# A two-block network on one core: weights' rests before operands' rests in the first ff product, shorter norms, and products of ones in the waits of two norms

## The reference, cut to what matters

```python
def rmsnorm(x, g):
    y = xf * lax.rsqrt(jnp.mean(xf * xf, axis=-1, keepdims=True) + EPS)
    return y * g
# first block
h = rmsnorm(x, norm_mix_g)                 # "n1"
...                                        # seven projections, gating, convolution
x = x + einsum(m, w_out)
hf = rmsnorm(x, norm_ff_g)                 # "n2"
z = relu(einsum(hf, w_ff1))                # 1024 -> 4096
x = x + einsum(z * z, w_ff2)               # 4096 -> 1024
x = rmsnorm(x, norm_final_g)               # "between"
# second block
mod = silu(c) @ w_ada + b_ada              # six vectors of 1024
h = rms_norm(x, g_norm1) * (1 + scale1) + shift1      # "n3"
...                                        # attention, gated linear attention, out projection
h2 = rms_norm(x, g_norm2) * (1 + scale2) + shift2     # "n4"
...                                        # gated mlp with a convolution
return rms_norm(x, g_final)                # "final"
```

## Time and profile before

| | |
|---|---|
| median of three runs | 1570.07 us (1569.48 to 1571.84) |
| the profiled execution | 1571.68 us, of which the span is 1569.9 us |
| busy, share of the span | PE 96%, weight loads 76%, DVE 51%, ACT 36%, POOL 2% |
| mean granted clock of PE | 0.973 of full |
| the chain that ended last | PE 89%, DVE 4%, ACT 3%, issue 2%, DMA 1% |

### The profile page before, as it was taken

How to read it: one execution, slowest core, us unless ns; L and a number is a source line. 1 busy time by engine, 2 the same in 40 slices (tenths; PEclk the granted TensorE clock), 3 DMA queues, 4 the chain that set the end, 5 groups by cost and what they waited for, 6 DMA issues and landing times.

```text
span 1569.9 us, 18627 instructions
## 1 busy us (share of the span) xinstructions
PE 1510.3 (96%) x6586; PEld 1198.4 (76%) x6586; DVE 804.0 (51%) x1108; ACT 562.6 (36%) x759; POOL 28.6 (2%) x68
## 2 busy tenths in 40 slices
PE   6999999999999999999997998999898999999997
PEld 5887888888887788888886764555686888888885
DVE  7344221652455656656677535445357552663564
ACT  4343222323233313232244333433435541551342
POOL 1000000000000000000000000000000000000000
PEclk7999999999999999999998999999898999999998
DMA  5333323233222553545344120110022233323221
GB/s 169 106 101 101 105 82 107 81 107 105 82 85 78 186 186 121 187 160 187 120 162 146 54 81 27 38 43 28 27 82 79 91 103 101 100 87 107 80 81 53
DMA packets 135788, 158.15 MB, mean 101 GB/s; under 512 B 2513, under 2 KB 129071, under 8 KB 135743
## 3 DMA queue, kind: packets, MB, share of 16 engines
q1 hardware_dynamic: 129024, 131.08, 25.9%
q0 software_dynamic: 6240, 26.30, 5.0%
q10 hardware_dynamic: 479, 0.17, 0.0%
HBM read 155.44 MB, written 2.10 MB: 100 GB/s over the span
## 4 chain that ended last, share of the span: by engine, by line
PE 89%; DVE 4%; ACT 3%; issue 2%; DMA 1%; DVEq 0%; SPq 0%; ACTq 0%
PE bank L395 27%; PE bank L397 27%; PE bank L396 27%; PE aux L637 1%; PE aux L632 1%; PE aux L653 1%; ACT weights_hi L693 1%; DMA gates<-in_x 1%; PE aux L435 1%; DVE ada_sums L1226 1%; PE aux L641 1%; DVE weights_lo L1001 1%; PE aux L416 1%; PE aux L509 1%; PE aux L581 0%
## 5 line engine op out<-in xcount | busy, mean ns | idle before, releaser
L395 PE MATMUL bank<-operand_hi,weights_hi 128*128 128x512 f32 x1936 | 768.0, 397 | 10.9 <-DVE operand_lo L1013 4.9
L396 PE MATMUL bank<-operand_lo,weights_hi 128*128 128x512 f32 x1936 | 757.8, 391 | 0.0
L397 PE MATMUL bank<-operand_hi,weights_lo 128*128 128x512 f32 x1936 | 757.6, 391 | 0.0
L395 PEld LDWEIGHTS bank<-operand_hi,weights_hi 128*128 128x128 f32 x1936 | 366.2, 189 | 109.6 <-issue 31.0
L397 PEld LDWEIGHTS bank<-operand_hi,weights_lo 128*128 128x128 f32 x1936 | 366.0, 189 | 77.1
L396 PEld LDWEIGHTS bank<-operand_lo,weights_hi 128*128 128x128 f32 x1936 | 366.6, 189 | 74.8 <-issue 1.0
L1001 DVE TENSOR_TENSOR weights_lo<-raw,weights_hi 128x1024 fp32r<-128x1024 f32 (+1 forms) x244 | 295.9, 1213 | 189.4 <-ACT weights_hi L693 182.8
L693 ACT ACTIVATE weights_hi<-raw 128x1024 fp32r<-128x1024 f32 (+1 forms) x244 | 253.1, 1043 | 182.0 <-PE bank L397 176.0
L1011 DVE TENSOR_TENSOR operand_lo<-value,operand_hi 128x512 f32 (+1 forms) x90 | 62.2, 692 | 94.8 <-ACT operand_hi L698 94.8
L698 ACT ACTIVATE operand_hi<-value 128x512 f32 (+1 forms) x90 | 56.9, 632 | 124.0 <-DVE value L1163 34.0
L1388 DVE SCALAR_TENSOR_TENSOR conv_or_gate<-bank,vector_table,conv_or_gate 128x511 f32<-128x511 f32 x44 | 32.9, 747 | 79.9 <-ACT conv_or_gate L959 78.1
(11 more groups left out here) (178 smaller groups left out, 749.6 us busy)
## 6 DMA issues: line engine op xcount, KB each, us to landing
raw<-in_w_in SPq DMA_DIRECT2D x40, 1024.0 KB, 5.1
raw<-in_w_ff SPq DMA_DIRECT2D x32, 1024.0 KB, 5.8
ada_or_attention<-in_w_ada POOLq DMA_DIRECT2D x16, 1536.0 KB, 7.5
raw<-in_w_up SPq DMA_DIRECT2D x22, 1024.0 KB, 5.1
raw<-in_w_out SPq DMA_DIRECT2D x8, 1024.0 KB, 5.0
raw<-in_w_down SPq DMA_DIRECT2D x8, 1024.0 KB, 5.0
raw<-in_w_proj_a SPq DMA_DIRECT2D x4, 1024.0 KB, 4.9
raw<-in_w_proj_b SPq DMA_DIRECT2D x4, 1024.0 KB, 5.0
```

The costliest lines, as they stand in the source:

```text
L395: pe.matmul(ps[k][:, :], wh, ah, start=(kt == 0), stop=False)
L396: pe.matmul(ps[k][:, :], wh, al, start=False, stop=False)
L397: mm = pe.matmul(ps[k][:, :], wl, ah, start=False, stop=(kt == k_tiles - 1))
```

## The change

1. **Order in part 0 of ff.** DVE makes the low part of the next weights ahead of the low part of the operand. ACT's program for this part stays as it is. The last chunk, and the `out` and `out2` phases, are written out on DVE rather than looped, since their last tile differs.
2. **Sums of squares.** In n1, n2, n3, n4 and final, DVE no longer adds the eighth square. PE sums over partitions first the seven added ones, then the eighth one itself, into the same columns: eight products of one column for four. The semaphore counts follow (`summed`). "between" keeps its form.
3. **Spread.** DVE's diagonals are gone. PE takes each block's reciprocals, one column broadcast to 128, against the identity: four products of 128 columns in place of one of 512.
4. **n2.** Sums and spread stand within the first ff pair, after its k-steps 0 to 2 and 3 to 5.
5. **Products of ones.** `keep_busy(n)` issues n fp32 products of `ones` with `gates[:, 0:512]` into `aux[2]`, whose result nobody reads: 3, 1 and 2 around n3's sums and spread, 2, 1 and 2 around n4's.

```diff
+        def summed(name, n):
+            whole = [m for m in SUM if SUM[m] < SUM[name]]
+            return sum(9 if m == "between" else 8 for m in whole) + n
...
             def sum_squares(norm):
+                if norm == "between":
+                    pe.wait_ge(sum_added, summed(norm, 9))
...
                 if norm == "n3":
-                    pe.wait_ge(sum3_added, 9)
-                    sums = ssum3
+                    pe.wait_ge(sum3_added, 8)
+                    sums, last = ssum3, sq3[1]
                 else:
-                    pe.wait_ge(sum_added, 9 * SUM[norm] + 9)
-                    sums = ssum[:, :]
+                    pe.wait_ge(sum_added, summed(norm, 8))
+                    sums, last = ssum[:, :], tb(1)
                 for b in range(NBLK):
-                    mm = pe.matmul(aux[0][:, b:b + 1], sums[:, b * P:(b + 1) * P], mean_w, start=True, stop=True)
+                    pe.matmul(aux[0][:, b:b + 1], sums[:, b * P:(b + 1) * P], mean_w, start=(b == 0), stop=False,
+                              skip_group_check=True)
+                if norm == "n3":
+                    pe.wait_ge(sq3_done, 8)
+                else:
+                    pe.wait_ge(sq_done, 8 * SUM[norm] + 8)
+                for b in range(NBLK):
+                    mm = pe.matmul(aux[0][:, b:b + 1], last[:, b * P:(b + 1) * P], mean_w, start=False,
+                                   stop=(b == NBLK - 1), skip_group_check=True)
                 mm.then_inc(norm_summed, 1)
 
+            def keep_busy(n):
+                for _ in range(n):
+                    pe.matmul(aux[2][:, :], ones[:, :], gates[:, 0:S], start=True, stop=True)
+
             def spread_rms(norm, bank=1):
-                pe.wait_ge(diag_done, NORM[norm] + 1)
-                pe.matmul(aux[bank][:, :], ones[:, :], spread[:, :], start=True, stop=True).then_inc(norm_spread, 1)
+                pe.wait_ge(inv_done, NORM[norm] + 1)
+                for b in range(NBLK):
+                    mm = pe.matmul(aux[bank][:, b * P:(b + 1) * P],
+                                   rms[:, NBLK + b:NBLK + b + 1].to_broadcast([P, P]), ident[:, :], start=True, stop=True)
+                mm.then_inc(norm_spread, 1)
...
                 q = F["ff"]
-                stream(q, (0, 1), 1, made(MADE["n2"]))
+                stream(q, (0, 1), 1, made(MADE["n2"]), first=0, last=3)
                 sum_squares("n2")
+                stream(q, (0, 1), 1, made(MADE["n2"]), first=3, last=6)
+                spread_rms("n2")
+                stream(q, (0, 1), 1, made(MADE["n2"]), first=6)
                 ada_turn(0)
-                stream(q, (2,), 1, first=0, last=4)
-                spread_rms("n2")
-                stream(q, (2,), 1, first=4)
-                stream(q, (3,), 1)
+                for k in (2, 3):
+                    stream(q, (k,), 1)
...
             ada_turn(16)
+            keep_busy(3)
             sum_squares("n3")
+            keep_busy(1)
             spread_rms("n3")
+            keep_busy(2)
...
+            keep_busy(2)
             sum_squares("n4")
+            keep_busy(1)
             spread_rms("n4")
+            keep_busy(2)
...
                 dve.reciprocal(rms[:, NBLK:2 * NBLK], rms[:, 0:NBLK]).then_inc(inv_done, 1)
-                dve.wait_ge(inv_done, NORM[name] + 1)
-                dve.tensor_tensor(spread[:, :].rearrange("p (b n) -> p b n", b=NBLK),
-                                  ident[:, :].unsqueeze(1).to_broadcast([P, NBLK, P]),
-                                  rms[:, NBLK:2 * NBLK].unsqueeze(2).to_broadcast([P, NBLK, P]),
-                                  ALU.mult).then_inc(diag_done, 1)
...
+            def ff_quad(c, part, i, last):
...
+                    dve.wait_ge(tile_done, 4 * q + k + 1)
+                    if part == 0:
+                        dve.wait_ge(value, VALUED["ff"] + KT * c + n - 1)
+                        dve.scalar_tensor_tensor(out=tb(k % 2), in0=ps[k][:, :], scalar=0.0, in1=spread[:, :],
+                                                 op0=ALU.max, op1=ALU.mult).then_inc(bank_read[k], 1)
+                        weights(q + 1, k)
+                        rest(0, n, tA[k % 2][:, :], MADE["ff"] + KT * c + n)
+                    else:
+                        grow_x(n, q, k)
+                        if not last:
+                            weights(q + 1, k)
```

More of the change, by code:

```diff
@@ L1124, in _, with quad, all_but_last_square, work @@
             dve.memset(acc[:, :], 0.0).then_inc(ada_step, 1)
+            def quad(name, i, work, after):
+                for k in range(4):
+                    q = F[name] + i
+                    if work is not None:
+                        dve.wait_ge(tile_done, 4 * q + k + 1)
+                        work(4 * i + k, q, k)
+                    if after is not None:
+                        after(4 * i + k, q, k)
+                    weights(q + 1, k)
             def phase(name, work, after=None, n=2):
                 with dve.Fori(0, n) as i:
[L1129 to L1136, removed]
+                    quad(name, i, work, after)
+            def all_but_last_square(name):
+                def work(n, q, k):
+                    if n < KT - 1:
+                        add_square(name, n, k % 2)
+                return work
             def product(dst, src):
@@ L1183, in split_x, with split_and_sum @@
                                          op1=ALU.subtract).then_inc(operand, 1)
[L1185 removed]
+            def split_and_sum(n, q, k):
                 dve.wait_ge(bank_read[k], q + 1)
                 split_x(n)
[L1188 to L1190 removed]
+                all_but_last_square("n2")(n, q, k)
+            for i in range(2):
+                quad("out", i, grow_x, split_and_sum)
             invert_rms("n2")
@@ L1192, in _ @@
             dve.wait_ge(n2_rms_kept, 1)
[L1194 to L1197, removed]
+            def ff_quad(c, part, i, last):
+                for k in range(4):
+                    q = F["ff"] + 4 * c + 2 * part + i
+                    n = 4 * i + k
+                    piece = 4 * c + 2 * part + i
+                    dve.wait_ge(tile_done, 4 * q + k + 1)
+                    if part == 0:
[7 more added lines that the diff above has]
+                        if not last:
+                            weights(q + 1, k)
+                    if k == 1:
+                        dve.wait_ge(ada_landed, 16 * (piece + 1))
+                        dve.wait_ge(ada_turned, piece + 1)
+                    if k in (1, 2):
+                        for kt in range(4 * (k - 1), 4 * k):
+                            src = ada_raw[:, kt * ADA:(kt + 1) * ADA]
+                            if kt == 0:
+                                dve.tensor_scalar(acc[:, :], src, cvec[:, kt:kt + 1], None, ALU.mult)\
+                                   .then_inc(ada_step, 1)
+                            else:
+                                dve.wait_ge(ada_step, 1 + KT * piece + kt)
+                                dve.scalar_tensor_tensor(out=acc[:, :], in0=src, scalar=cvec[:, kt:kt + 1],
+                                                         in1=acc[:, :], op0=ALU.mult, op1=ALU.add)\
+                                   .then_inc(ada_step, 1)
+                    if last and part == 1:
+                        add_square("between", n, k % 2)
+                        if n < KT - 1:
+                            dve.wait_ge(sq3_done, n + 1)
+                            dve.wait_ge(sum3_added, n + 1)
+                            dve.tensor_tensor(ssum3, ssum3, sq3[k % 2], ALU.add).then_inc(sum3_added, 1)
+                        weights(q + 1, k)
@@ L1198, in ff_chunk @@
+            def ff_chunk(c):
                 for part in range(2):
                     with dve.Fori(0, 2) as i:
[L1200 to L1213, removed]
[L1214 to L1234 removed]
```

52 lines of the change are left out of this document (21 added, 31 removed).

## The result

The changed kernel takes 1604.87 us (median of 4 runs, 1603.86 to 1606.61) against 1570.95 us (4 runs, 1569.48 to 1574.99): 1.0213 times as long, 95% interval 1.0191 to 1.0235. The profiled execution took 1605.6 us over a span of 1603.8, against 1571.68 and 1569.9; so 33.9 us of span are to be explained. The forecast was 1598 us, range 1586 to 1610. The kernel before was timed again beside the experiments: medians of 1572.24 to 1575.00 us, single runs from 1569.27 to 1577.18.

The account below looks back on a forecast made before the run. PE, busy 96% of the span, was taken as the bound: its work plus its waits. Stalls 27.8, clock 8.0 and norms -7.6 gave +28.2 us on the profiled 1571.68, 1599.9; less 1.6 to the median, 1598 us, range 1586 to 1610.

Parts of the forecast that it names:

- Step of a tile on DVE: Part 0 of ff: the new order costs DVE 0.95 us a tile in the loop, 0.75 in the last chunk.
- Stalls: PE waits in the four ff chunks: 5.6 us in the first, 8.0 each in two, 6.2 in the last; 27.8 together.
- the old 3.6 us: First ff chunk before the change: PE's waits of 2.0 us for low weights and 1.59 us for a low operand.
- The clock after the waits: After each of the four ff waits PE's clock falls to half, costing 2.0 us each (0 to 3.4), 8 together.
- Norms: Shorter norms: n3 and n4 gain 3.2 us each, final 1.2, n1 0; together -7.6, between -2.5 and -10.
- the one in which the clock holds in ff: Same ff stalls, but the clock holds or its fall costs nothing: 1590 us, chance 0.2.
- The one in which the products of ones don't hold the clock: n3 and n4 keep a gain of only 0.74 us each: 1603 us, chance 0.15.
- The rival on the other side: DVE in part 0 of ff: low weights are ready sooner and nothing is lost; 1560 us, chance 0.06.

Follow-up runs that it names:

- The order alone: Kernel before the change, with only DVE's two steps in part 0 of ff swapped, low weights ahead of low operand: 1607.09 us, ratio 1.0212.
- the run without products of ones: The changed kernel with all calls of `keep_busy` left out: 1605.11 us.
- the run with six products: The changed kernel with 6 products of ones in each of the four long ff waits, ahead of the last k-step: 1588.2 us.

## Why the prediction came out, point by point

The sign, the mechanism and the place were right, and the time lay in the range, 6.9 us above the forecast. Two terms were off in opposite directions, the stalls by 4.4 us and the clock by 9.7; that the total came so near is in part luck.

- **Step of a tile on DVE.** Forecast 0.95 us; from the low operand's start to the next own work it is 0.92 (530.55 to 531.47 in the first chunk). Low weights 3.15 us after the bank is read, low operand 4.29: both as forecast.
- **Stalls.** Forecast 27.8 us net. Measured: 1.45 + 5.76 us in the first chunk, 1.39 + 5.80 in the second, 1.38 + 5.82 in the third, 5.44 in the fourth, 27.0 in all. But the old 3.6 us are to be taken off, which leaves 23.4. The chunks gave 3.6, 7.2, 7.2 and 5.4 where I had 5.6, 8.0, 8.0 and 6.2. The first was most off: its first bank was read at 494.95, not near 496.2, so its last k-step came at 546.40, not 547.9.
- **The clock after the waits** is the term that was mis-sized: 8.0 forecast, 17.7 measured behind the waits, of which filling them gave back 16.0 by the quads' starts. The step that failed is "I take 2.0 for each, as the n4 wait is nearest in length", with an upper end of 3.4. The order alone gave just 2.0 a time, the changed kernel 3.9 to 4.8 (and once 1.8, in the run without products of ones), after waits of nearly the same length. By the figure in the Trainium skill (TensorE: Matmul & The Clock Gate, section on HAM oscillation), 1.67 us throttled and half of it lost, an estimate for all four would have been 3.3. No run here agrees: no fall after a whole wait cost less than 1.8 us.
- **Norms.** Forecast -7.6, measured about -8.0: n4 -3.1 (forecast -3.2), n3 -2.2 with the mixer behind it (-3.2), final -2.3 (-1.2; its spread ran at full clock, 1.16 us, though no products of ones stand there), n1 -0.4 (0). Two of these are in part luck: n3 held its clock in only three of the nine traces with products of ones (worth 0.9 us), and the final spread took 1.16 us in four of the ten traces with this final norm, 1.44 to 1.93 in the others.
- **Sum.** 23.4 + 17.7 - 8.0, and 0.6 more in the first chunk, where the longer sums now lie inside the pair, make 33.7 of the 33.9 us of the spans.

Of the rivals, the one in which the clock holds in ff is false here; the run with six products makes it true, at 1588.2 us, forecast 1590. The one in which the products of ones don't hold the clock is refuted by the windows of this execution and for n4 by every trace; for n3 it is what six traces of nine show. In the whole their gain shows only where the stalls are gone. The rival on the other side needs ACT's high weights to end first; moved there, they give 1559.68, forecast 1560.

## What to carry to other kernels

When two steps of one engine each wait for another engine, order them as the other engine delivers; swapping them on one side alone turned time that was waited out anyway into a step per tile, and moving the producer's side as well repaired it. Price a stall of TensorE as the wait and then the clock, by rows at half clock from several places, and give the second term a wide range: here it was between 1.8 and 4.8 us for nearly the same wait. And take the length of a filler product (one whose result nobody reads) from its own row: 22 of them cost 37 us more than none, where six gained 16.7.

## What the runs showed of the hardware

- After idleness of 5.8 us the clock stood at half for 6.8 us in one kernel and for 10.4 in another, at the same place of the program; the run without products of ones has both, the longer in its second chunk (0.74 over 640 to 660) and the shorter in its third (0.83 over 740 to 760). After 3.1 us it fell in two of four cases. The length of the wait alone does not set the price; what does was not found.
- Products whose results nobody reads can hold the clock, but they don't always. With them the granted clock stayed at 1.00 in n4 in all nine traces, in the four ff waits with six products each, and in the final norm in the one trace that has them there. In n3 it stayed in three traces of nine and fell in six, behind the same products and the same waits.
- A plain fp32 product of 128x512 stands as two records and takes 0.865 us at full clock (44 records in 19.04 us), 3.8 times the 0.2264 us of one product of rounded halves.
- The mixer's own time varied between 271.4 and 275.6 us among kernels whose mixer is the same, with its short clock falls at other places each time. A gain of 3 us elsewhere can vanish in it.
